# Where the mixers' and the experts' buffers begin in SBUF, in a two-layer hybrid encoder

## What is computed

```python
for l in range(DEPTH):                     # DEPTH = 2
    mix = hybrid_mixer(x, w_in[l], w_out[l], ...)
    x = layer_norm(DEEPNORM_ALPHA * x + mix, ln1_g[l], ln1_b[l])
    f = swiglu(x, ...) if l % 2 == 0 else moe_swiglu(x, ...)
    x = layer_norm(DEEPNORM_ALPHA * x + f, ln2_g[l], ln2_b[l])

def swiglu(x, w_gate, w_up, w_down):
    return (jax.nn.silu(x @ w_gate) * (x @ w_up)) @ w_down
```

## Time and profile before

| | |
|---|---|
| median of 3 runs | 1332.92 us (1327.78 to 1335.93) |
| the profiled execution | 1329.73 us |
| its span, first to last instruction | 1327.7 us |
| TensorE busy | 1250.4 us, 94% |
| VectorE, ScalarE, GpSimd busy | 904.4, 707.4, 58.3 us |
| mean granted TensorE clock | 0.945 |
| moved by DMA | 300.13 MB, mean 226 GB/s |

### The profile page before, as it was taken

The page is one execution under the profiler, slowest core; times in us unless marked ns, Lnnn a source line. Parts: engine busy times, 40 slices in busy tenths (PEclk is TensorE's granted clock), DMA queues, the critical chain, the costliest instruction groups (busy, mean ns, idle before and its releaser), DMA issues.

```text
span 1327.7 us, 14942 instructions
## 1 busy us (share of the span) xinstructions
PE 1250.4 (94%) x5856; PEld 1028.4 (77%) x5856; DVE 904.4 (68%) x840; ACT 707.4 (53%) x721; POOL 58.3 (4%) x47
## 2 busy tenths in 40 slices
PE   7897999999998999499999999999999999999994
PEld 6676878887876788488888888878888888777883
DVE  3657465444466664568888767878877798886673
ACT  4445344433344452166776655766765576775550
POOL 2200020000042000000000000000000000000000
PEclk9896799999998958599999999999999999999997
DMA  9921165554565000198889888898888889888750
GB/s 294 321 96 64 42 211 192 164 210 165 190 179 193 1 1 0 69 356 305 306 296 317 287 320 280 302 331 312 291 291 317 309 288 323 298 309 289 299 192 35
DMA packets 126788, 300.13 MB, mean 226 GB/s; under 512 B 4938, under 2 KB 7128, under 8 KB 126704
## 3 DMA queue, kind: packets, MB, share of 16 engines
q1 hardware_dynamic: 124304, 291.52, 63.3%
q0 software_dynamic: 2112, 6.87, 1.8%
q10 hardware_dynamic: 288, 0.63, 0.1%
HBM read 297.88 MB, written 1.12 MB: 225 GB/s over the span
## 4 chain that ended last, share of the span: by engine, by line
PE 82%; DVE 6%; issue 4%; ACT 3%; DMA 2%; POOL 2%; DVEq 0%; POOLq 0%; SPq 0%; ACTq 0%
PE bank L1360 19%; PE bank L1361 19%; PE bank L1418 13%; PE bank L1705 12%; PE bank L1446 6%; PE bank L1718 6%; ACT w_hi L601 2%; DMA raw<-in_w_in 1%; PE bank L1669 1%; DVE soft L932 1%; PE bank L1566 1%; PE bank L1685 1%; DVE w_lo L860 1%; DVE neg_max L933 1%; POOL w_lo L558 1%
## 5 line engine op out<-in xcount | busy, mean ns | idle before, releaser
L860 DVE TENSOR_TENSOR w_lo<-raw,w_hi 128x2048 fp32r<-128x2048 f32 x273 | 620.9, 2290 | 319.1 <-ACT w_hi L601 317.7
L601 ACT ACTIVATE w_hi<-raw 128x2048 fp32r<-128x2048 f32 x275 | 523.9, 1917 | 322.8 <-PE bank L1418 161.6
L1360 PE MATMUL bank<-w_hi,xT_hi 128*128 128x512 f32 (+1 forms) x896 | 353.0, 395 | 8.0 <-DVE xT_lo L872 3.2
L1361 PE MATMUL bank<-w_hi,xT_lo 128*128 128x512 f32 (+1 forms) x896 | 348.5, 390 | 0.0
L1418 PE MATMUL bank<-w_lo,xT_hi 128*128 128x512 f32 (+1 forms) x832 | 219.7, 387 | 0.0
L1360 PEld LDWEIGHTS bank<-w_hi,xT_hi 128*128 128x128 f32 x896 | 171.0, 191 | 44.1 <-ACT xT_hi L612 6.1
L1361 PEld LDWEIGHTS bank<-w_hi,xT_lo 128*128 128x128 f32 x896 | 171.0, 191 | 34.2
L1418 PEld LDWEIGHTS bank<-w_lo,xT_hi 128*128 128x128 f32 x832 | 154.6, 189 | 33.0 <-DVE w_lo L860 1.0
L1360 PE MATMUL bank<-w_hi,hT_hi 128*128 128x512 f32 x312 | 123.7, 397 | 1.8 <-issue 1.8
L1361 PE MATMUL bank<-w_hi,hT_lo 128*128 128x512 f32 x312 | 123.0, 394 | 0.0
L1705 PE MATMUL bank<-w_hi,xs 128*128 128x512 f32 x336 | 94.3, 402 | 0.0
(11 more groups left out here) (208 smaller groups left out, 1004.5 us busy)
## 6 DMA issues: line engine op xcount, KB each, us to landing
raw<-in_moe_w_gate SPq DMA_DIRECT2D x70, 1024.0 KB, 5.4
raw<-in_moe_w_up SPq DMA_DIRECT2D x70, 1024.0 KB, 5.5
raw<-in_moe_w_down SPq DMA_DIRECT2D x70, 1024.0 KB, 5.4
raw<-in_w_in SPq DMA_DIRECT2D x24, 1024.0 KB, 8.5
raw<-in_ffn_w_gate SPq DMA_DIRECT2D x11, 1024.0 KB, 5.1
raw<-in_ffn_w_up SPq DMA_DIRECT2D x11, 1024.0 KB, 5.2
raw<-in_ffn_w_down SPq DMA_DIRECT2D x11, 1024.0 KB, 5.0
raw<-in_w_out SPq DMA_DIRECT2D x8, 1024.0 KB, 5.0
```

What stands on the lines that cost most here:

```text
L601: nc.scalar.activation(w_hi[:, n % NH, :], raw[:, n % NR, :], ACT.Copy).then_inc(hi_done, 1)
L860: nc.vector.tensor_tensor(w_lo[:, n % NH, :], raw[:, n % NR, :], w_hi[:, n % NH, :].bitcast(F32), ALU.subtract).then_inc(lo_done, 1)
L1360: nc.tensor.matmul(o, hi, wh, start=start, stop=False)
L1361: nc.tensor.matmul(o, lo, wh, start=False, stop=False)
```

## The change

line_pad grows from 32 to 160 bytes a partition. Everything allocated after it moves up by 128 bytes: proj, qk_hi, qk_lo, bias_c, soft, hT_hi, hT_lo, xs, hs, hid_s, sel and selT begin at 128 modulo 256. raw, w_hi, w_lo, xtok, xT_hi, xT_lo, row, acc and tab stay. No instruction is added, removed or put elsewhere.

```diff
@@ -203,7 +203,7 @@
         lam_sum = sb("lam_sum", [P, 2])
         lam_exp = sb("lam_exp", [P, 2])
         lam_neg = sb("lam_neg", [P, 1])
-        line_pad = sb("line_pad", [P, 8])
+        line_pad = sb("line_pad", [P, 40])
 
         with ExitStack() as s:
             proj = sb("proj", [P, NT, QKV], scope=s)
```

## The result

The change takes the median from 1327.78 to 1317.14 us (seven runs each): a ratio of 0.9916, 95% interval 0.9894 to 0.9937. The profiled execution has a span of 1314.7 us where before had 1327.7. I forecast a gain of 10.4 us; the medians lie 10.6 us apart, the ratio says 11.2, the two profiled spans 13.0.

The account below looks back on a forecast made before the run. TensorE's matmul starts were taken to bound the experts and dense feed-forward. Terms of 4.7 and 6.1 us, less 0.4 for short blocks, gave 10.4 us: 1332.9 to 1322.5 us, forecast's range 1319 to 1327, 8 in 10 1316 to 1333.

Parts of the forecast that it names:

- What bounds the kernel: Experts and dense feed-forward: time is the number of matmuls times the distance between two starts; transfers wait for compute.
- the three short distances in the scatter: L1727, selT stationary and hs moving, both at 0: last three starts 227 ns each, settling after a start-up.
- Rival A: Distance follows something else, the upper half of SBUF or the stage; nothing changes, 1333 us; chance 0.16.
- The hT term: 936 matmuls with hT stationary go from 231.7 to 226.7 ns, 5.0 ns each: 4.7 us gained.
- The term of xs and hs: 1008 matmuls with xs or hs stationary go from 232.8 to 226.7 ns, 6.1 ns each: 6.1 us gained.
- The start-ups: 0.05 us per block: some 45 xs, hs, hT blocks lose 2.2 us, some 43 xT blocks gain 2.2; they cancel.
- The small matmuls at 0: Transposes, gather and scores going to equal places: taken as 0, bounds 3.0 us gained or lost.
- Rival D: More than forecast: small matmuls gain 3.0 us and start-ups vanish (2.2 us); 16 us gained, 1317 us; chance 0.07.
- Rival B: Only hT settles, as its slices step by 1024 bytes, those of xs and hs by 512; 1328 us; chance 0.10.
- Rival C: Slower: position table's pieces straddle 256-byte blocks, landing 8.9 us later; 7 us lost, 1340 or 1330 us; chance 0.04.
- either way: Second layer: GpSimd's add on the position table holds up a VectorE instruction, lam_prod or the w_lo split.
- VectorE's splits at 2290 ns: Sign to look for in the profile after: VectorE's splits unchanged at 2290 ns.

Follow-up runs that it names:

- All at 0: Kernel before with padding so that weights, xT and the stage buffers all begin at 0 modulo 256: 1317.36 us beside 1328.34, ratio 0.9912.
- all moved together: Kernel before with all buffers moved by 128 bytes, weights and xT at 0, stage buffers at 128 modulo 256: 1326.4 us, ratio 0.9991.
- The mixers alone: Kernel before with only the mixers' buffers (proj, qk, soft, bias_c, small ones) moved by 128 bytes: 1328.45 us, ratio 1.0002.
- w_lo apart: Kernel before with w_lo, xtok, xT, row, acc, tab moved to 0 and stage buffers to 128 modulo 256, w_hi staying at 128: 1336.04 us.

## Why the prediction was right, point by point

- What bounds the kernel: right. TensorE waits for nobody in the experts after as before, and its saving went through to the end; the weights came faster as it asked for them.
- The reading of the three short distances in the scatter, equal places far up in SBUF: right, and it was the row that told the two explanations apart. All at 0 and all moved together confirm it from both sides. Rival A falls. The Trainium skill's "TensorE: Matmul & The Clock Gate", section "Step-by-step: what each phase is for", says that loading the next stationary operand takes no read bandwidth from the running matmul; the distances of these matmuls don't bear that out, as the place of the one operand relative to the other costs 5 ns in 227. The runs show the rule of the places; that the two reads get in each other's way is an inference.
- The hT term, 5.0 ns by 936: measured 5.4 ns; 1.27 us in the dense feed-forward where 264 x 5.0 is 1.3, and 2.88 alone in the experts where 672 x 5.0 is 3.4.
- The term of xs and hs, 6.1 us: a little large. Their blocks are short and many follow a transposition, so their mean goes to 228.1 and not to 226.7: 1008 x 4.7 = 4.7 us. The 4.55 us measured alone are those of the whole stage, with what the other blocks gain or lose by them.
- The start-ups: I let 2.2 us lost and 2.2 gained cancel, and neither is what I said. The first eight matmuls of the 43 xT blocks behind xs or hs take 79.05 us before and 78.41 after: 0.6 us gained. On the other side the moved operands end at 228.1, 228.0 and 227.0 ns and not at 226.7, which over 1008 and 936 matmuls is about 1.7 us not gained. Together, 9.6 us from the two stages against my 10.4.
- The small matmuls at 0: no effect seen. The mixers alone have a ratio of 1.0002 (0.9990 to 1.0015). In the experts the transposes of hid_s stand 97.2 ns apart before and 97.0 after, the gather's matmuls 135.2 and 135.2 (means of distances under 300 ns), which were among the groups that I had priced at up to 5 ns each. Rival D's mechanisms fall, although its time of 1317 us is what was measured: its 16 us had been subtracted from 1332.9, a median 5.1 us above that of seven runs.
- Rival B falls: xs and hs settle with steps of 512 bytes.
- Rival C: if the mechanism exists, it is worth half a microsecond in place of 8.9. I took the row of the whole transfer for the price of its pieces. The Trainium skill's "DMA: Bandwidth & Descriptors", section "How a descriptor splits into AXI transactions", speaks of extra data fetched for a start off the 256-byte boundary, on the reading side; the landing of 9.4 to 10.1 us against 8.6 to 9.4 agrees in sign, with few profiles. The hold-up of VectorE by GpSimd's add, "either way", which I used in C, is what all fourteen profiles show, and the order around it is worth 2 us.
- VectorE's splits at 2290 ns: their mean is 2303 after the change. The median is unchanged at 2291; two splits that lie over the position table's adds take 3.93 and 4.92 us, where before one took 2.92.

The sum of the stages explains 9.6 of the 10.6 to 11.2 us; what is left is inside the interval and the open part above. So the mechanism was right and its size within a tenth, but that the medians differ by 10.6 us, so near to the forecast's 10.4, is partly luck.

## What to carry to other kernels

Let the stationary and the moving operand of a dense stream of matmuls begin at the same place modulo 256 bytes, all of them in the stream: here it is 5 ns in 227, 2%, for 128 bytes of padding, measured for matmuls of 512 columns with a new stationary operand each. To find it, compare starts, not durations, of two groups that differ in nothing but the tensor, and look at the allocator's addresses when they differ by a few nanoseconds. A group in which one half agrees gains little: with w_lo apart xs stood at 231.6 ns, where it has 232.7 before and 228.1 after the change.

## What the runs showed that I had not expected

- The effect has no slope. 32 bytes off costs as much as 128 (233.2 ns against 232.4), 256 bytes off nothing (227.0), and 192 is half way (229.6).
- Places that agree for part of a block leave most of it slow: with w_lo apart no group had a mean under 229 ns, although 1992 of 4536 weight matmuls had agreeing places, and the one run took 1336.0 us.
- A VectorE product of 64 columns lasts 0.22 or 5.13 us, by whether it starts 0.4 us before (the change) or 0.63 us after (before) an add on GpSimd that reads SBUF. The Trainium skill, "SBUF — State Buffer", section "Who interferes with whom", says that a VectorE instruction with two SBUF inputs contends with a GpSimd instruction that reads SBUF, and calls the contention an exclusive lock; the trace agrees, as the product ends with the add.
- Which instruction is held can matter more than how long. The add holds the product for 5.13 us before and the scaling of gain_a for 4.88 with the mixers alone, and yet the first row maximum comes 2.2 us sooner in the latter, because ScalarE's next step no longer stands behind the hold-up.
